# Widening the up products of a streamed mixture of experts from 256 to 512 columns, and adding their halves inside the turn that follows

## The reference, cut to what matters

```python
def _moe(h, gates, w1, w3, w2):
    y = jnp.zeros_like(h)
    for e in range(N_EXPERTS):
        a = jax.nn.silu(h @ w1[e]) * (h @ w3[e])
        y = y + gates[..., e:e + 1].astype(h.dtype) * (a @ w2[e])
    return y
```

## Time and profile before

| | us |
|---|---|
| median of 3 runs | 1263.22 |
| lowest and highest | 1261.59, 1272.76 |
| the profiled execution, its own time | 1269.81 |
| its span (first to last instruction) | 1268.0 |
| mean granted TensorE clock in it | 0.908 of 2.4 GHz |

### The profile page before, as it was taken

One profiled execution on the slowest core, in us unless ns is written; L12 is line 12 of the kernel. 1 busy time (PEld: TensorE's weight loads), 2 busy tenths in 40 slices (PEclk: granted clock), 3 DMA queues, 4 the chain that ended last, 5 costly groups with the idle time before them and its releaser, 6 DMA issues.

```text
span 1268.0 us, 24266 instructions
## 1 busy us (share of the span) xinstructions
PE 1025.1 (81%) x9133; PEld 567.7 (45%) x9134; DVE 336.0 (26%) x787; ACT 227.2 (18%) x559; POOL 257.6 (20%) x483
## 2 busy tenths in 40 slices
PE   4999998899999989978775769998997748745860
PEld 1544756444645545544342434555444425423430
DVE  1002217423433212111110146116233201110114
ACT  0211117501411101101010123116122001100100
POOL 1000000100064333332221320000001313312431
PEclk9799999899899999998797859999997879988995
DMA  9993310380647666688999997321876999999952
GB/s 297 407 409 143 133 67 1 120 312 1 265 168 268 235 230 236 232 309 331 350 361 401 387 367 271 115 84 67 300 315 246 370 404 399 381 391 406 387 189 101
DMA packets 91140, 331.40 MB, mean 261 GB/s; under 512 B 12828, under 2 KB 15068, under 8 KB 66516
## 3 DMA queue, kind: packets, MB, share of 16 engines
q1 hardware_dynamic: 68532, 282.13, 58.4%
q0 software_dynamic: 21088, 47.48, 10.7%
q10 hardware_dynamic: 1472, 1.12, 0.3%
HBM read 303.17 MB, written 27.53 MB: 261 GB/s over the span
## 4 chain that ended last, share of the span: by engine, by line
PE 66%; DMA 16%; issue 9%; DVE 4%; ACT 3%; SPq 2%; POOL 0%; POOLq 0%; DVEq 0%; ACTq 0%
PE PS L1632 18%; PE PS L1434 17%; DMA W<-in_moe_w 13%; PE PS L1648 8%; PE PS L1551 7%; PE PS L1380 3%; PE PS L1622 3%; PE PS L1399 2%; DMA W<-in_w_ada 2%; PE PS L1640 2%; PE PS L1601 1%; ACT EX L789 1%; DMA H<-y_rows,DEST 1%; PE PS L1370 1%; PE PS L1562 1%
## 5 line engine op out<-in xcount | busy, mean ns | idle before, releaser
L1632 PE MATMUL PS<-W,EX 128*32 128x256 f32 x4224 | 280.4, 422 | 114.3 <-DMA W<-in_moe_w 64.9
L1632 PEld LDWEIGHTS PS<-W,EX 128*32 128x32 f32 x4224 | 151.3, 121 | 222.2 <-issue 153.3
L1434 PE MATMUL PS<-W,XT 128*128 128x512 f32 (+1 forms) x544 | 219.8, 565 | 3.1 <-ACT XT L722 3.1
L1434 PEld LDWEIGHTS PS<-W,XT 128*128 128x128 f32 x544 | 104.4, 194 | 112.7 <-issue 110.3
L1648 PE MATMUL PS<-W,AT 128*32 128x256 f32 x2112 | 131.0, 389 | 1.5 <-DVE AT L1267 1.5
L692 ACT ACTIVATE AT<-EX 64x512 f32<-64x512 f32 x64 | 40.4, 631 | 446.8 <-PE PS L1622 442.5
L1260 DVE COPY EX<-PS 128x256 f32<-128x256 f32 x66 | 28.0, 425 | 342.7 <-PE PS L1632 342.7
L588 POOL TENSOR_TENSOR RSTD<-VAR,HALF 128x1 f32<-128x1 f32 (+1 forms) x24 | 16.3, 683 | 482.1 <-DVE VAR L968 482.1
L619 POOL DMA_DIRECT2D y_rows<-AT x136 | 67.5, 499 | 207.9 <-DVE AT L1270 198.2
L619 POOL DMA_DIRECT2D y_rows<-EX x128 | 63.5, 496 | 166.2 <-DVE EX L1270 145.7
L1551 PE MATMUL PS<-W,XT 128*128 128x512 f32 x192 | 85.0, 603 | 0.0
(11 more groups left out here) (192 smaller groups left out, 842.3 us busy)
## 6 DMA issues: line engine op xcount, KB each, us to landing
W<-in_moe_w SPq DMA_DIRECT2D x96, 2048.0 KB, 14.1
W<-in_w_ada SPq DMA_DIRECT2D x24, 2048.0 KB, 14.6
W<-in_w_in SPq DMA_DIRECT2D x8, 2048.0 KB, 26.4
EX<-xg_rows POOLq DMA_DIRECT2D x136, 64.0 KB, 5.8
W<-in_w_out SPq DMA_DIRECT2D x4, 2048.0 KB, 9.9
xg_rows<-X POOLq DMA_DIRECT2D x1, 6656.0 KB, 30.9
y_rows<-X POOLq DMA_DIRECT2D x1, 4608.0 KB, 44.2
y_rows<-AT POOLq DMA_DIRECT2D x136, 32.0 KB, 5.2
```

What stands on the lines that cost most here:

```text
L1434: mm = pe.matmul(ps[:, 0:cw], XT[:, k, P * t:P * t + P], w[:, k, :], start=(k == 0), stop=(k == KD - 1))
L1632: mm = pe.matmul(UP_PS[o:o + ROWS, 0:256], rows, moe_up(3 * p + n)[:, k, 256 * a:256 * a + 256], start=(k == 0), stop=(k == KD - 1), tile_ ...
```

## The change: what it does

`up` no longer halves the 512 columns. For each piece k and each matrix n it issues one matmul with 512 moving columns, and even and odd k go to different column tiles: partitions 32(2n + k%2). So the four tiles hold, for each matrix, the sum over even pieces and the sum over odd pieces, each 512 wide. That makes 16 matmuls in place of 32, and UP_PS is 512 columns wide in place of 256. `copy_up` copies all 512. `turn_act` becomes four ordinary matmuls: stationary is a 128x128 strided quarter of EXU, moving a constant 128x64 matrix of zeros and ones, `pair`, that adds the even and the odd part of each row while turning. The layouts of w2 in its slot (one 16 KB run per partition in place of two of 8 KB), of GU, ATX and EXU follow, and XGT moves to the tile R4. The constant table grows by 64 columns (32 KB).

```diff
@@ constants
+    pair = np.zeros((P, 2 * ROWS))
+    for n in range(2):
+        for odd in range(2):
+            for r in range(ROWS):
+                pair[ROWS * (2 * n + odd) + r, ROWS * n + r] = 1
@@ views
-        EXU = EX[:, 0, 0:256]
-        GU = EX[:, 3, 0:4 * ROWS].rearrange("p (k s) -> p k s", k=2)
-        XGT = EX[:, 0, 256:256 + 8 * ROWS].rearrange("p (k s) -> p k s", k=4)
-        ATX = AT[:, 0, 0:4 * ROWS].rearrange("p (k s) -> p k s", k=2)
+        EXU = EX[:, 0, :]
+        GU = EX[:, 3, 0:4 * ROWS].rearrange("p (k s) -> p k s", k=4)
+        XGT = R4[:, 0, 0:8 * ROWS].rearrange("p (k s) -> p k s", k=4)
+        ATX = AT[:, 0, 0:4 * ROWS].rearrange("p (k s) -> p k s", k=4)
@@ moe_load
-                k = 4 if n < 2 else 2
-                dst = W[:, s, :].rearrange("p (q x) -> p q x", q=2)
+                q = 2 if n < 2 else 1
+                dst = W[:, s, :].rearrange("p (q x) -> p q x", q=q)
...
@@ copy_up
-                    dve.tensor_copy(EXU, UP_PS[:, 0:256]).then_inc(up_copied[L], 1)
+                    dve.tensor_copy(EXU, UP_PS).then_inc(up_copied[L], 1)
@@ up
                     for k in range(KD):
                         rows = XGT[:, k % 4, ROWS * (k // 4):ROWS * (k // 4) + ROWS]
                         for n in range(2):
-                            for a in range(2):
-                                o = ROWS * (2 * n + a)
-                                mm = pe.matmul(UP_PS[o:o + ROWS, 0:256], rows,
-                                               moe_up(3 * p + n)[:, k, 256 * a:256 * a + 256],
-                                               start=(k == 0), stop=(k == KD - 1), tile_position=(0, o))
+                            o = ROWS * (2 * n + k % 2)
+                            mm = pe.matmul(UP_PS[o:o + ROWS, :], rows, moe_up(3 * p + n)[:, k, :],
+                                           start=(k < 2), stop=(k >= KD - 2), tile_position=(0, o))
                     mm.then_inc(up_done[L], 1)
@@ turn_act
-                    turned = EXU.rearrange("s (f k) -> s k f", k=2)
-                    for k in range(2):
-                        mm = pe.transpose(TURN_PS[:, P * k:P * k + P], turned[:, k, :], IDENT)
+                    parts = EXU.rearrange("s (f k) -> s k f", k=4)
+                    for k in range(4):
+                        mm = pe.matmul(TURN_PS[:, 2 * ROWS * k:2 * ROWS * k + 2 * ROWS], parts[:, k, :], cst("pair"),
+                                       start=True, stop=True)
                     mm.then_inc(act_turned[L], 1)
@@ down
-                        rows = ATX[:, k % 2, ROWS * (k // 2):ROWS * (k // 2) + ROWS]
...
-                            mm = pe.matmul(DOWN_PS[o:o + ROWS, 0:256], rows,
+                            mm = pe.matmul(DOWN_PS[o:o + ROWS, 0:256], ATX[:, k, :],
```

More of the change, by code:

```diff
@@ L235, in constants @@
             sel[32 * j + r, r] = 1
-    parts = {"ident": np.eye(P), "cn": two(cn), "sn": two(sn), "cc": blk(np.cos(a64)), "sc": blk(np.sin(a64)),
+    pair = np.zeros((P, 2 * ROWS))
[3 more added lines that the diff above has]
+                pair[ROWS * (2 * n + odd) + r, ROWS * n + r] = 1
+    parts = {"pair": pair, "ident": np.eye(P), "cn": two(cn), "sn": two(sn), "cc": blk(np.cos(a64)), "sc": blk(np.sin(a64)),
              "rc": two(rc), "rs": two(rs), "sel": sel,
@@ L494, in moe_load @@
                 s = 3 * e + n
-                k = 4 if n < 2 else 2
-                dst = W[:, s, :].rearrange("p (q x) -> p q x", q=2)
+                q = 2 if n < 2 else 1
+                dst = W[:, s, :].rearrange("p (q x) -> p q x", q=q)
                 src = (moe_w1, moe_w3, moe_w2)[n][L, at, :, :]
-                src = src.rearrange("(q p k) n -> p q (k n)", q=2, p=P) if isinstance(at, int) else \
-                    src.rearrange("o (q p k) n -> p (o q) (k n)", q=2, p=P)
+                src = src.rearrange("(q p k) n -> p q (k n)", q=q, p=P) if isinstance(at, int) else \
+                    src.rearrange("o (q p k) n -> p (o q) (k n)", q=q, p=P)
                 sp.dma_start(dst, src).then_inc(w_full[s], 16)
@@ L853, in gate @@
                 def gate():
-                    h = TURN_PS[:, 0:8 * ROWS].rearrange("p (k c s) -> p k c s", k=2, c=2)[:, :, 0, :]
+                    h = TURN_PS[:, 0:8 * ROWS].rearrange("p (k c s) -> p k c s", k=4, c=2)[:, :, 0, :]
                     nc.scalar.activation(GU, h, ACT.Silu).then_inc(gate_ready[L], 1)
@@ L1265, in product @@
                 def product():
-                    h = TURN_PS[:, 0:8 * ROWS].rearrange("p (k c s) -> p k c s", k=2, c=2)[:, :, 1, :]
+                    h = TURN_PS[:, 0:8 * ROWS].rearrange("p (k c s) -> p k c s", k=4, c=2)[:, :, 1, :]
                     dve.tensor_tensor(ATX, h, GU, ALU.mult).then_inc(product_ready[L], 1)
```

## The result

The changed kernel takes 1301.5 us (median of 4 runs, 1294.2 to 1304.9) against 1263.7 before: a ratio of 1.028, with a 95% interval of 1.0239 to 1.0322. I had forecast 1271 with a range up to 1286. The direction was right, the size was a quarter of what came, and the time lies outside the range. The profiled execution took 1294.2 us (span 1292.4) and is the fastest of the four; the one of before (1269.8) was on the slow side of its runs. So the two traces differ by 24.4 us, less than the medians' 37.9.

A forecast was written before the change was run, and what follows sets the result against it. TensorE's stream bounds the experts before 640, weights by DMA mostly after. First layer +7.7 (+16.8 less 9.1) and +0.5, second layer 0: +8.2, 1278.0 us for the profiled execution, 1271.4 on the median; range 1257 to 1286.

The forecast's parts named there:

- Up, 3.56 us: Up product in each expert step: 16 matmuls of twice the width take 3.56 us against 3.59, a gain of 0.03.
- turn_act, 0.98 us, between 0.84 and 1.02: Turn in each expert step: eight records in place of two, priced from similar rows at 0.98 us, +0.54 a step.
- The rule on the transpose mode: turn_act: FP32 transpose mode is four times as fast; leaving it would give 1.76 us, +1.3 a step, some +43 us.
- Steps that end in a hole before up: 11 of 33 steps, sequencer late: longer copy +0.27 and 12 more instructions +0.28, less 0.03; 0.51 us used for all.
- Holes before turn_rows close: Experts' first steps: up's 64 instructions are handed out sooner, so every such hole should close, -9.1 us before 636.8.
- The copy and w2's runs cost nothing: copy_up, 0.27 us longer, lies beside turn_rows and down; w2's packets stay below either run length; both cost nothing.
- The DMA stream absorbs the second layer's delays: Second layer's experts: delays up to 1162 are absorbed by the never-empty weight stream; the 8 steps behind net 0.
- my +7.7: First layer up to the filled DMA stream: 33 steps at 0.51 make +16.8, less 9.1 of closed holes.
- +8.2 us on 1269.8: Forecast total for the profiled execution: first layer +7.7 and +0.5, second layer 0, giving 1278.0 us.
- (a): Rival: holes before turn_rows stay, 44 steps at 0.51 or 0.53 add +22 to +23, 1286 us; chance 0.20.
- (b): Rival: holes before up shrink by a quarter with the smaller loop body, -9.2 us, 1262 us; chance 0.12.
- (c): Rival: three ups behind holes of 2.4 to 3.2 us and one slow down stay at 2.4 GHz, 1264; chance 0.10.

The follow-up runs named there:

- contig: Changed kernel, each turn_act product reading 128 neighbouring columns of EXU, w2 laid out to match in four 4 KB runs; ratio 1.0056 to the kernel before, 1271.1 us.
- copy_permutes: Changed kernel with w2's layout kept; VectorE's copy_up writes EXU sorted by quarter, so turn_act reads neighbouring columns; ratio 1.0019 to the kernel before.
- turn4_t16: Changed kernel with four transposes at a 16-byte step in turn_act, even and odd parts added afterwards on VectorE; ratio 0.993 to the kernel before, 1258.3 us.
- turn_alone: Kernel before, its two turn_act transposes made ordinary products with the identity at a step of 8 bytes; ratio 1.0058 to the kernel before.
- late_sequencer: Wide up and copy, old two transposes over half the up result, plus two unused META loads in each expert's first step; ratio 0.9914 to the kernel before.
- up_alone: Changed kernel's wide up and copy, with the old two transposes over half the up result, the rest left out; ratio 0.9892 to the kernel before, 1249.8 us.

## Why the prediction was wrong, point by point

- *Up, 3.56 us.* Right: 3.57. The array streamed before and streams after.
- *turn_act, 0.98 us, between 0.84 and 1.02.* This step failed. I took L1364 and L1491 as the nearest rows because the shape of the stationary operand and the type agreed (of L1364 only these: it moves 2 columns, not 64), and did not ask whether the operand was laid out alike. Both read neighbours; the new turn reads every fourth element, and costs 2.01 us. Without the step (contig, copy_permutes) the term is 1.04, still a little above my upper bound. The trace of before had no ordinary product with such a stationary operand, only transposes (turn_rows reads at 16 bytes), and turn4_t16 shows that these don't pay for it. So no row showed this operation, and its upper bound should have stood open.
- *The rule on the transpose mode.* By it I had 1.76 us, against 0.98 by the row, and went with the row. 1.76 is nearer to 2.01, but for another reason: at a step of 8 bytes the same exchange costs 0.67 against 0.44 us (turn_alone), not four times as much. The Trainium skill (TensorE: Matmul & The Clock Gate, LDWEIGHTS) gives the time of a load, in ns, as its columns divided by 1.2, whatever the number of rows; for 128 columns that is 107 ns. These traces agree at a step of 8 bytes, where four records more, with as many moving columns in all, cost 1.09 - 0.67 = 0.42 us, 105 ns each (the profile's load records are longer, 196 ns, and overlap), and not at 16, where each of the eight records costs (2.01 - 1.04) / 8 = 0.12 us more than at 4.
- *Steps that end in a hole before up.* The mechanism was right, and it shielded the kernel: a hole of 4.07 us is 2.8 to 2.9 after, so there the dear turn runs beside the sequencer's tests. Of the 1.57 us that the turn grew by, 1.15 are hidden in such a step, and it grew by 0.40 us, where I had 0.51.
- *Holes before turn_rows close.* Right: 9.1 us became 0.3 up to the same point of the first layer, META is reached after 1.7 us, and late_sequencer brings holes back.
- *The copy and w2's runs cost nothing.* Right: all waits for L1265 together are 0.4 us on PE's matmuls, and the intervals of contig (w2 in runs of 4 KB) and copy_permutes (16 KB) overlap.
- *The DMA stream absorbs the second layer's delays.* Right: from that layer's first up to the expert that starts at 1162.35 before and at 1180.02 after, it takes 193.8 and 194.1 us.

The sum with the right term, first layer. With 1.54 in place of 0.51 us in the 22 steps without a hole, my +7.7 becomes +30.4. The traces show +26.9 from the first up to the 35th (277.7 us before, 304.6 after), and the steps of both account for it. 24 of these 34 have no long hole behind them, +1.54 each: +37.0. The ten that end in a hole of 1.5 us or more grew by 0.40: +4.0. Closed holes before turn_rows: -8.8. Short holes before the first ups, closed too: -1.0. The ups behind the last three long holes, 5.0 us in place of 6.3 (granted clock 0.72 against 0.57): -3.9. The clock elsewhere: -0.7. Together +26.6. The part that the weights bind, up to the third-last step, gave 2.1 back, and the last three steps took 3.0 more, 1.7 of it in one down at the lower clock (3.6 us in place of 1.9): with these it is the 27.9 of above, to a rounding.

In the second layer 8 steps at 1.54 are 12.3, less 3.5 by which the three holes before up shrank, less 3.9 of closed holes: 4.9. One up and the last down ran 1.4 us longer each at the lower clock (6.42 against 5.04, 3.31 against 1.93): 7.7 in all, where 7.8 - 0.3 = 7.5 came behind 1162.35.

With a contiguous operand the forecast stands: +8.2 us on 1269.8, a ratio of 1.0065, against 1.0056 (1.0026 to 1.0086) in contig.

Of the rivals, (a) didn't happen; its 1286 was the nearest number, for a wrong reason. (b) didn't either: up_alone has the smaller loop body too, with the turn of before, and its holes before up are as long as ever. Instructions in order of time, up_alone:

```profile
551.92 6.10 PE L1636 MATMUL PS<-W,R 128*32 128x512 f32 x32 [3.97 <-issue]
```

(c) happened in part. Of the three ups and the down that it names, the first up and the down ran at 2.4 GHz after (3.64 and 1.93 us, granted clock 1.00); the other two ups did not. Two other ups cancelled that: they took 3.66 us before at a granted clock of 1.00, and 5.34 after at 0.68, with no long hole before them. And the 3.9 us of the last three ups above are the clock's too, at ups that (c) doesn't name. Instructions in order of time, the changed kernel:

```profile
359.03 5.34 PE L1636 MATMUL PS<-W,R 128*32 128x512 f32 x32
...
393.53 5.34 PE L1636 MATMUL PS<-W,R 128*32 128x512 f32 x32 [0.37 <-issue]
...
428.88 3.64 PE L1636 MATMUL PS<-W,R 128*32 128x512 f32 x32 [1.31 <-issue]
```

Nor does the length of the hole decide alone: in up_alone that first hole is 2.42 us, as before, and the up behind it takes 3.64 us at a granted clock of 1.00, where it took 5.35 at 0.69. What moved the clock stays open. All this is a few microseconds beside 35.7. What I had written down as a sign of error, a turn_act above 1.2 us, is what came.

## What to carry to other kernels

A row prices an operation only if the layout of each operand agrees too, not shape and type alone; where no row does, leave that bound open. For a float32 stationary operand with a step above 8 bytes, sort the data in the copy that comes before it anyway (VectorE did so for nothing) or use transposes. And where TensorE's sequencer is late, fewer and wider instructions can pay, although the array's own time is the same.

## What the runs showed of the hardware that I had not expected

- An ordinary float32 product with 128 stationary columns costs 0.105 us a record at a step of 8 bytes. Taking off the 1.09 - 8 x 0.105 = 0.25 us that stands once, my estimate is 0.10 at 4 bytes, 0.16 at 12 and 0.22 at 16. Four transposes cost 0.68 us at 8 and at 16 bytes alike.
- VectorE reads PSUM in float32 at a step of 16 bytes as fast as neighbours: 691 ns for 512 columns either way.
- TensorE's sequencer hands out a weight load or matmul in 23 to 27 ns at the full clock (3.0 us for 128, 1.7 us for 64), read from how long after an up's start it reaches META. Where the up ran wholly or partly at 1.2 GHz, that took 4.2 to 5.5 us for 128 and 2.5 to 3.0 us for 64, 33 to 47 ns each. up_alone, with 64 instructions fewer in a step, nearly the same time of the array and no holes before turn_rows, is 1.1% faster.
